# Delta rule in a one-core block: block coefficients and decay rows copied through DRAM, one direction solved from its far end, two substitutions in turn

## The chip, the cores and the metric

The kernel runs on 1 core of one Trainium2 chip, in one launch. The metric is the device time in microseconds. A core has TensorE (PE, weight loads PEld), VectorE (DVE), ScalarE (ACT), GpSimd (POOL) and SyncE (SP), and 16 DMA engines. The granted TensorE clock was 0.999 of full speed over the whole profiled run.

## What is computed

Two transformer blocks in a row over 256 tokens of 2048 channels, in float32. The second block mixes with a gated delta rule and a Fourier branch, and the change lies in the delta rule. Per head (8 heads, both directions, chunks; the kernel takes each 128 tokens as a chunk):

```
diff = gc[..., :, None] - gc[..., None, :]          # gc: running sum of the log decays g
decay = jnp.where(incl, jnp.exp(jnp.where(incl, diff, 0.0)), 0.0)
m = jnp.where(strict, jnp.einsum("bhnid,bhnjd->bhnij", kb, k) * decay, 0.0)
a_mat = m + jnp.eye(CHUNK, dtype=m.dtype)
sol = lax.linalg.triangular_solve(a_mat, rhs, left_side=True, lower=True, unit_diagonal=True)
qk = jnp.where(incl, jnp.einsum("bhnid,bhnjd->bhnij", q, k) * decay, 0.0)
...
o_b = flip(gated_delta_rule_chunked(flip(q), flip(k), flip(v), flip(g_b), flip(beta_b)))
```

The triangular matrix of 128 is inverted in 16x16 blocks on the diagonal by substitution on VectorE, and these are joined in three levels (32, 64, 128) by matmuls.

## The kernel before

**The stream.** Nearly all of the time is matmuls with streamed weights. A unit is 128x1024 weights (512 KB): SP loads it to `raw` (one of 4 slots; the slot is free when POOL has done with it), ACT copies it rounded to `w_hi` (line 678, once PE has finished the unit 4 before), POOL writes the rest to `w_lo` (line 637), PE multiplies both (lines 2201 and 2204).

**The pairs.** The 8 heads run in 4 pairs, `p` = 0 to 3; the two heads of a pair are `ways[0]` ("one") and `ways[1]` ("other"). Each has two PSUM banks, `x_ps` and `y_ps`; its four 128x128 matrices are 2 directions by 2 chunks. In a pair PE also works through 28 units of the stream, `fill(n)` being n half units, set by hand between the steps of the pair. DVE adds up each finished group of 4 units (`group_out`, lines 1830 to 1833), which frees its bank for the group after next.

**A pair, in the order of its chain.** Convolution on DVE (line 1889), silu on ACT, transposes on PE (`to_tokens`), norms on ACT (`norms`, line 1120, ending in `vt`, line 1126) and the copy of the keys, `ks`, on DVE (line 1895). Then the steps that the change touches:

- `log_sums` on PE (line 2686): a matmul with one column of `gc_head` and the rows `gc_rows` puts gc of every token on all partitions; `log_decay` on DVE takes gc of the row off it, and adds the mask; `decays` on ACT (line 1142) takes the exponential, after `betas` of both ways.
- `grams` on PE (line 2693): the products k k and q k. They wait for `ks` of their way.
- `matrices` on DVE: product with decay (line 1912), q k and level-4 masks (1914, 1918), blocks masked (1916) and summed into rows of 16 (1921), the diagonal added (1923), and these spread out by 4 products (1928, 1930).
- `spread` on PE (lines 2699, 2701): matmuls with the 0/1 matrix `same` give every partition the 16x16 coefficients of its block, in PSUM.
- `substitution` on DVE (lines 1942, 1944): for n = 1 to 15 a product and a sum for one way, each waiting for the one before, then the same for the other way; then each way's expansion and transposes (1947, 1951, 1956).
- `level` on PE (line 2720), which waits for `tt1`, the last transpose of its way; later levels, solves, states and outputs follow, with short fills between.

Every engine works through its list in order, so what stands behind a wait waits too. ACT's list holds the `w_hi` copies 3 to 30 of the pair between its own steps.

Of the kernel before, what the change touches and what calls it, by code (L numbers as in the profile page):

```python
# [18 lines left out]
F32 = mybir.dt.float32  # L19
# [7 lines left out]
P = 128  # L27
T = 256
# [175 lines left out]
def build(nc, t, out):  # L204
    ctx = ExitStack()
    with ctx:
# [15 lines left out]
        def rounds(name, names):  # L222
# [33 lines left out]
        same = own[:, 768:896]  # L256
# [6 lines left out]
        gc_rows = b[:, 7, :, :].rearrange("p s n -> p (s n)")  # L263
        gc_head = b[:, 6, 0, 0:HN]
# [22 lines left out]
        out_done = sem("out_done")  # L287

# [63 lines left out]
        mk_dve = steps("mk_dve", ["a", "b", "c", "s", "same", "neg", "nth", "which", "pick0", "pick", "sel0", "sel"])  # L352
        sc_pe = steps("sc_pe", ["feat", "scal", "cum", "rows"])
        sc_act = steps("sc_act", ["whi", "ea", "b0", "b1", "e", "ln", "eg", "er", "rowhi"])
        sc_dve = steps("sc_dve", ["wlo", "feat", "a0", "a1", "neg", "abs", "pos", "sp", "nea", "g0", "g1", "zero", "gc", "rem", "rowlo", "ne"])
# [6 lines left out]
                        + ["one", "ks", "rn", "dsub", "dmin", "m0", "m1", "m2", "m3", "qk", "blk", "mm4", "red", "dl", "r0", "r1", "r2", "r3"]  # L362
                        + [y for n in range(1, BASE) for y in (f"pr{n}", f"su{n}")] + ["cp", "ex0", "ex1", "tt0", "tt1"]
                        + [f"l{l}{n}" for l in (4, 5) for n in range(4)] + ["u60", "u61", "vd0", "vd1", "v10", "v11", "ra", "rb", "v20", "v21",
                                                          "o", "orn", "on", "ot", "lo"]) for w in range(2)]
        dn_act = [steps(f"dn_act{w}", ["sqk", "sv", "n0", "n1", "n2", "n3", "root", "vt0", "vt", "r2", "be0", "be", "qe", "exp", "mc", "x4", "x5", "x6",
                                       "s", "qs0", "qs1", "os0", "os1", "oroot0", "oroot", "hi"]) for w in range(2)]
        dn_pe = [steps(f"dn_pe{w}", ["tr1", "gc", "gram", "mbx", "mby", "x4", "tu4", "x5", "tu5", "x6", "tu6",
# [44 lines left out]
        class Way:  # L413


            def __init__(self, w, two, both):
# [12 lines left out]
                self.low_rows, self.top_rows = both[:, 0:4 * HALF * BASE], both[:, 4 * HALF * BASE:6 * HALF * BASE]  # L429
# [4 lines left out]
                self.inv = own[:, 64 * w:64 * w + 64].rearrange("p (n i) -> p n i", n=4)  # L434
                self.prod = own[:, 128 + 64 * w:192 + 64 * w].rearrange("p (n i) -> p n i", n=4)
# [230 lines left out]
        def _(act):  # L666
# [387 lines left out]
            for g in range(FG):  # L1054
# [37 lines left out]
                if g == 6:  # L1092
                    act.wait_ge(sc_pe.sem, sc_pe.at("rows"))
                    act.wait_ge(sc_dve.sem, sc_dve.at("zero"))
                    nc.scalar.activation(gc_rows[0:HN], ps[0:HN, 0, :], ACT.Copy).then_inc(sc_act.sem, 1)

            for p in range(PAIRS):
# [123 lines left out]
                for w in ways:  # L1221
                    out_norms(w)
                fill(28, 29, 30)
# [44 lines left out]
        def _(dve):  # L1268
# [514 lines left out]
            nc.vector.tensor_tensor(same, in_block[:, 0], in_block[:, 1], ALU.add).then_inc(mk, 1)  # L1783
            dve.wait_ge(mk, done("s"))
            nc.vector.tensor_tensor(same, same, ident[:], ALU.add).then_inc(mk, 1)
# [7 lines left out]
            nc.vector.tensor_scalar(gc_head, ident[:, 0:HN], 1.0, None, ALU.mult).then_inc(mk, 1)  # L1793
            dve.wait_ge(mk, done("sel0"))
            nc.vector.tensor_scalar(gc_head[32:64], ident[32:64, 32:32 + HN], 1.0, None, ALU.mult).then_inc(mk, 1)
# [39 lines left out]
            for g in range(FG):  # L1835
# [7 lines left out]
                if g == 2:  # L1843
                    nc.vector.memset(gc_rows.bitcast(F32), 0.0).then_inc(sc_dve.sem, 1)
# [4 lines left out]
                if g == 6:  # L1849
                    dve.wait_ge(sc_act.sem, sc_act.at("rowhi"))  # L1850
                    nc.vector.tensor_tensor(gc_rows[32:40], ps[0:HN, 0, :], gc_rows[0:HN].bitcast(F32), ALU.subtract).then_inc(sc_dve.sem, 1)
# [7 lines left out]
            for p in range(PAIRS):  # L1859
# [39 lines left out]
                def log_decay(w):  # L1899
                    own, y = dn_dve[w.w].sem, four1(w.y_ps)  # L1900
                    from_pe(w, "gc")
                    nc.vector.tensor_tensor(y, y, per(GC, w), ALU.subtract).then_inc(own, 1)
                    after(w, "dsub")
                    nc.vector.scalar_tensor_tensor(out=y, in0=y, scalar=0.0, in1=dmask[:], op0=ALU.min, op1=ALU.add).then_inc(own, 1)

                def matrices(w):
# [7 lines left out]
                    nc.vector.tensor_tensor(dc(w.qk), two(w.x_ps[:, T:2 * T]), dc(w.decay), ALU.mult).then_inc(own, 1)  # L1914
                    after(w, "m3")
                    nc.vector.tensor_tensor(dc(w.x), dc(y), in_block.unsqueeze(2).broadcast_to([P, 2, 2, P]), ALU.mult).then_inc(own, 1)
                    after(w, "qk")
                    nc.vector.tensor_tensor(dc(w.mm4), dc(y), lmask[:, 4].unsqueeze(2).broadcast_to([P, 2, 2, P]), ALU.mult).then_inc(own, 1)
                    after(w, "blk")
                    sums = w.x_ps[:, 0:64].rearrange("p (n i) -> p n i", n=4)  # L1920
                    nc.vector.tensor_reduce(sums, w.x.rearrange("p n (b i) -> p n i b", i=BASE), AX.X, ALU.add).then_inc(own, 1)
                    after(w, "red")
                    nc.vector.tensor_tensor(sums, sums, nth.unsqueeze(1).broadcast_to([P, 4, BASE]), ALU.add).then_inc(own, 1)
                    after(w, "dl")
                    for rows, cols, part in ((slice(HALF, BASE), BASE, w.low_rows), (slice(0, HALF), HALF, w.top_rows)):
                        place = part.rearrange("p (d c o q) -> p d c o q", d=2, c=2, o=HALF)
                        wide = [P, 2, HALF, cols]
                        nc.vector.tensor_tensor(place[:, 0], sums[:, 0:2, rows].unsqueeze(3).broadcast_to(wide),
                                                nth[:, 0:cols].unsqueeze(1).unsqueeze(1).broadcast_to(wide), ALU.mult).then_inc(own, 1)
                        nc.vector.tensor_tensor(place[:, 1], sums[:, 2:4, 0:cols].unsqueeze(2).broadcast_to(wide),  # L1930
                                                nth[:, rows].unsqueeze(2).unsqueeze(1).broadcast_to(wide), ALU.mult).then_inc(own, 1)

                def substitution(w):

                    own = dn_dve[w.w].sem
                    low = w.x_ps.rearrange("p (n o q) -> p n o q", n=4, o=HALF)
                    top = w.y_ps[:, 0:4 * HALF * HALF].rearrange("p (n o q) -> p n o q", n=4, o=HALF)
                    coef = lambda n: top[:, :, n, 0:n + 1] if n < HALF else low[:, :, n - HALF, 0:n + 1]
# [107 lines left out]
                for w in ways:  # L2046
                    matrices(w)
# [823 lines left out]
```

## Time and profile before

| | us |
|---|---|
| median of 3 runs | 2162.88 (2162.18 to 2163.45) |
| the profiled run | 2162.75 |
| its span, first to last instruction | 2160.9 |
| PE busy | 2147.3 (99%) |
| POOL busy | 1710.2 (79%) |
| DVE busy | 1088.4 (50%) |
| ACT busy | 1041.4 (48%) |
| the four pairs, about | 884 to 1268 |

Times in the rows are us from the start of the span. A row of the timeline is one instruction, or several alike in a row (x and their number), with its start and how long it took; an idle time of its engine of over 0.2 us stands in brackets, with what ended it. Matmuls overlap, so what a step costs PE is read from start to start, not from the durations.

### The profile page before, as it was taken

The numbers are of one execution on the slowest core, as the hardware profiler recorded it, in microseconds if no ns is written. First come the engines' busy times: TensorE is split into PE (matmuls) and PEld (weight loads), VectorE is DVE, ScalarE is ACT, GpSimd is POOL, SyncE is SP. The second block draws the span as 40 slices with busy tenths as digits, with TensorE's granted clock in tenths as the row PEclk, the third lists the DMA queues.
The fourth block names the chain that finished last, engine by engine and source line by source line (L and its number), as shares of the span: only waits on it lengthen the run. The fifth ranks groups of instructions, "written<-read, shape, count | busy, mean of one in ns | idle before, by whom it ended". The sixth has DMA issues, their size and how long they took to land.

```text
span 2160.9 us, 35017 instructions
## 1 busy us (share of the span) xinstructions
PE 2147.3 (99%) x12871; PEld 1847.3 (85%) x12871; DVE 1088.4 (50%) x1887; ACT 1041.4 (48%) x1533; POOL 1710.2 (79%) x729
## 2 busy tenths in 40 slices
PE   9999999999999999999999999999999999999998
PEld 8888889888888888888888888888888888888886
DVE  5994343115754253668686745118506704822842
ACT  5434455444567556646455654453333333333343
POOL 7888868877666886667676768888888888888886
PEclk9999999999999999999999999999999999999999
DMA  7666545656454765555565546656666666666664
GB/s 247 186 189 191 177 154 175 190 156 186 146 145 146 236 181 148 141 155 166 138 174 138 157 150 200 206 184 189 190 194 189 191 194 188 191 192 190 191 189 153
DMA packets 321604, 383.84 MB, mean 178 GB/s; under 512 B 14942, under 2 KB 255941, under 8 KB 321221
## 3 DMA queue, kind: packets, MB, share of 16 engines
q1 hardware_dynamic: 317269, 378.06, 58.8%
q10 hardware_dynamic: 4208, 4.00, 0.6%
q8 instruction: 90, 1.47, 0.3%
q14 instruction: 37, 0.30, 0.0%
HBM read 379.92 MB, written 2.10 MB: 177 GB/s over the span
## 4 chain that ended last, share of the span: by engine, by line
PE 97%; DVE 1%; issue 1%; ACT 1%; POOL 0%; ACTq 0%; POOLq 0%; DVEq 0%
PE lin_ps L2201 37%; PE lin_ps L2204 18%; PE lin_ps L2228 10%; PE lin_ps L2229 10%; PE lin_ps L2227 10%; PE ps L2164 1%; PE lin_ps L2411 1%; PE lin_ps L2409 1%; PE lin_ps L2410 1%; PE ps L2554 0%; DVE ps L1889 0%; POOL w_lo L637 0%; PE lin_ps L2340 0%; PE lin_ps L2341 0%; PE lin_ps L2339 0%
## 5 line engine op out<-in xcount | busy, mean ns | idle before, releaser
L637 POOL TENSOR_TENSOR w_lo<-raw,w_hi 128x1024 fp32r<-128x1024 f32 (+1 forms) x712 | 1699.2, 2396 | 426.2 <-ACT w_hi L678 318.0
L2201 PE MATMUL lin_ps<-a,w_hi 128*128 128x512 f32 x2176 | 695.0, 401 | 1.1 <-DVE a L1299 0.4
L678 ACT ACTIVATE w_hi<-raw 128x1024 fp32r<-128x1024 f32 (+1 forms) x452 | 471.1, 1053 | 450.4 <-PE lin_ps L2204 236.6
L2204 PEld LDWEIGHTS lin_ps<-a,w_lo 128*128 128x128 f32 x2176 | 408.7, 188 | 96.4
L2201 PE MATMUL lin_ps<-b,w_hi 128*128 128x512 f32 x1376 | 432.7, 396 | 0.8 <-DVE z L1534 0.8
L2204 PE MATMUL lin_ps<-a,w_lo 128*128 128x256 f32 x2176 | 428.4, 278 | 0.0
L689 ACT ACTIVATE w_hi<-raw 128x1024 fp32r<-128x1024 f32 x228 | 242.0, 1062 | 385.6 <-PE lin_ps L2204 226.4
L2201 PEld LDWEIGHTS lin_ps<-a,w_hi 128*128 128x128 f32 x2176 | 332.9, 189 | 5.5 <-issue 2.5
L2204 PEld LDWEIGHTS lin_ps<-b,w_lo 128*128 128x128 f32 x1376 | 258.5, 188 | 61.0
L2227 PE MATMUL lin_ps<-w_hi,a 128*128 128x512 f32 x752 | 293.3, 390 | 0.0
L2229 PE MATMUL lin_ps<-w_hi,a 128*128 128x512 f32 x752 | 292.7, 389 | 0.0
L2228 PE MATMUL lin_ps<-w_lo,a 128*128 128x512 f32 x752 | 292.6, 389 | 0.0
L2204 PE MATMUL lin_ps<-b,w_lo 128*128 128x256 f32 x1376 | 270.4, 278 | 0.0
L2201 PEld LDWEIGHTS lin_ps<-b,w_hi 128*128 128x128 f32 x1376 | 209.8, 189 | 1.9 <-DVE z L1534 1.3
L2229 PEld LDWEIGHTS lin_ps<-w_hi,a 128*128 128x128 f32 x752 | 141.2, 188 | 29.1
L2227 PEld LDWEIGHTS lin_ps<-w_hi,a 128*128 128x128 f32 x752 | 141.2, 188 | 29.0
L2228 PEld LDWEIGHTS lin_ps<-w_lo,a 128*128 128x128 f32 x752 | 141.2, 188 | 28.9
L1319 DVE SCALAR_TENSOR_TENSOR x<-lin_ps,nst,x 128x512 f32<-128x512 f32 x24 | 16.9, 747 | 219.6 <-PE lin_ps L2229 219.6
L2116 DVE TENSOR_TENSOR a<-scr,a 128x512 f32 x32 | 92.3, 2884 | 4.7
L1426 DVE SCALAR_TENSOR_TENSOR ps<-z,vec,ps 128x254 f32<-128x254 f32 (+28 forms) x232 | 88.4, 465 | 0.0
L2112 DVE SCALAR_TENSOR_TENSOR scr<-scr 128x512 f32<-128x512 f32 x32 | 86.8, 2714 | 1.1
L2114 DVE CAST a<-scr 128x512 f32 x32 | 78.2, 2444 | 5.1 <-DVE scr L2112 5.1
(440 smaller groups left out, 2136.7 us busy)
## 6 DMA issues: line engine op xcount, KB each, us to landing
raw<-in_w_in SPq DMA_DIRECT2D x144, 512.0 KB, 3.7
raw<-in_w_mlp_up SPq DMA_DIRECT2D x128, 512.0 KB, 3.8
raw<-in_w_mlp_down SPq DMA_DIRECT2D x128, 512.0 KB, 3.7
raw<-in_even_w_in SPq DMA_DIRECT2D x111, 512.0 KB, 3.6
raw<-in_odd_w_in SPq DMA_DIRECT2D x40, 512.0 KB, 3.7
raw<-in_even_w_out SPq DMA_DIRECT2D x32, 512.0 KB, 4.2
raw<-in_odd_w_out SPq DMA_DIRECT2D x32, 512.0 KB, 4.8
raw<-in_w_o SPq DMA_DIRECT2D x32, 512.0 KB, 4.3
```

The costliest lines, as they stand in the source:

```text
L637: nc.gpsimd.tensor_tensor(w_lo[:, slot, 0:width], raw[:, slot, 0:width], w_hi[:, slot, 0:width].bitcast(F32), ALU.subtract).then_inc(lo_do ...
L678: nc.scalar.activation(w_hi[:, slot, 0:width], raw[:, slot, 0:width], ACT.Copy).then_inc(hi_done, 1)
L689: nc.scalar.activation(w_hi[:, slot], raw[:, slot], ACT.Copy).then_inc(hi_done, 1)
L1426: nc.vector.scalar_tensor_tensor(out=acc[c][:, k:T], in0=u[c][:, 0:T - k], scalar=per_channel(w + 8 * (TAPS - 1 - k) + c), in1=acc[c][:, k:T],
L2112: nc.vector.scalar_tensor_tensor(out=tm2, in0=tmp, scalar=0.0, in1=tmp, op0=ALU.max, op1=ALU.mult).then_inc(ml_dve.sem, 1)
L2114: nc.vector.tensor_copy(bb[:, :, 0, :], tm2).then_inc(ml_dve.sem, 1)
L2116: nc.vector.tensor_tensor(bb[:, :, 1, :], tm2, bb[:, :, 0, :].bitcast(F32), ALU.subtract).then_inc(ml_dve.sem, 1)
L2201: nc.tensor.matmul(lin_ps[:, 2 * parity + m, :], hi[:, k, m * P:(m + 1) * P], src[:, kk].rearrange("p s n -> p (s n)"), start=(q == 0 and ...
L2204: last = nc.tensor.matmul(lin_ps[:, 2 * parity + m, 0:T], lo[:, k, m * P:(m + 1) * P], src[:, kk, 0, :], start=False, stop=(q == n - 1 and ...
L2227: nc.tensor.matmul(acc, ah, hi[:, k, :], start=(j == 0 and k == 0), stop=False)
L2228: nc.tensor.matmul(acc, ah, lo[:, k, :], start=False, stop=False)
L2229: last = nc.tensor.matmul(acc, al, hi[:, k, :], start=False, stop=(j == 7 and k == 1))
```

## The change

It replaces the matmuls that spread data over partitions by copies through DRAM. The cumulative log decays are written once to `gc_far` (8 rows of 512) and read back for each way, broadcast to 128 partitions (256 KB). The block rows are written to `co_far` (32 KB a way and pair) and read back so that the 16 partitions of a block all hold its 16 rows (512 KB, into the former `tu` space, now `coef`). `log_sums`, `spread`, the two helpers `gc_rows` and `gc_head`, and the four spreading products go. PE's fills 2, 9 and 13 become one of 24. One direction is solved from its last row back, so that both directions read the same rows; the sums, the inverse and the products lie in PSUM. On DVE `scales` and `log_decay` alternate by way, `group_out` of a group moves behind the coefficients of both ways, and the two substitutions alternate step by step. On ACT `decays` of the first way moves ahead of `betas`.

```diff
@@ ACT @@
+                    nc.scalar.activation(scr[0:HN, 3, :], ps[0:HN, 0, :], ACT.Copy).then_inc(sc_act.sem, 1)
+                    act.wait_ge(sc_act.sem, sc_act.at("rows"))
+                    act.dma_start(gc_far, scr[0:HN, 3, :]).then_inc(gc_out, 16)
...
+                def decay_rows(w, k):
+                    act.dma_start(w.x.rearrange("p a n -> p (a n)"),
+                                  gc_far[2 * k + w.w:2 * k + w.w + 1, :].broadcast_to([P, 4 * P])).then_inc(gc_in[w.w], 16)
+                def coefs_out(w):
+                    from_dve(w, "dl")
+                    act.dma_start(co_far[w.w], w.rows.rearrange("p n i -> p (n i)")).then_inc(co_out[w.w], 16)
+                def coefs_in(w):
+                    act.wait_ge(co_out[w.w], 16 * (p + 1))
+                    act.dma_start(w.coef, co_far[w.w].rearrange("(b o) f -> b (o f)", o=BASE).unsqueeze(1)
+                                  .broadcast_to([P // BASE, BASE, 4 * BASE * BASE])).then_inc(co_in[w.w], 16)
...
                     act.wait_ge(bld, 4)
+                    act.wait_ge(gc_out, 16)
+                    for w in ways:
+                        decay_rows(w, 0)
...
                 norms(other)
+                decays(one_way)
                 betas(one_way)
                 fill(9)
                 betas(other)
-                decays(one_way)
+                decays(other)
                 fill(10, 11)
-                decays(other)
+                coefs_out(one_way)
                 fill(12)
+                coefs_out(other)
+                fill(13)
+                coefs_in(one_way)
                 keep_m(one_way)
-                fill(13, 14)
                 keep_m(other)
+                coefs_in(other)
+                fill(14)
...
+                if p < PAIRS - 1:
+                    for w in ways:
+                        decay_rows(w, p + 1)
@@ DVE @@
+                    dve.wait_ge(gc_in[w.w], 16 * (p + 1))
+                    from_act(w, "vt")
+                    for n in range(4):
+                        nc.vector.tensor_scalar(y[:, n, :], w.x[:, n, :], col(GC, n // 2, n % 2, w), 0.0, ALU.subtract, ALU.min).then_inc(own, 1)
+                    after(w, "dsub3")
+                    nc.vector.tensor_tensor(y, y, dmask[:], ALU.add).then_inc(own, 1)
...
+                    nc.vector.tensor_reduce(w.sums, w.x.rearrange("p n (b i) -> p n i b", i=BASE), AX.X, ALU.add).then_inc(own, 1)
+                    after(w, "red")
+                    nc.vector.tensor_tensor(w.rows, w.sums, nth.unsqueeze(1).broadcast_to([P, 4, BASE]), ALU.add).then_inc(own, 1)
...
+                def substitutions():
+                    for w in ways:
+                        dve.wait_ge(co_in[w.w], 16 * (p + 1))
+                    for n in range(1, BASE):
+                        far = BASE - 1 - n
+                        for w in ways:
+                            after(w, f"su{n - 1}" if n > 1 else "one")
+                            nc.vector.tensor_tensor(window(w.prod, 0, 2 * BASE, n + 1),
...
+                        for w in ways:
+                            after(w, f"pr{n}")
+                            nc.vector.tensor_reduce(window(w.inv, far, 2 * BASE - far + n, 1), window(w.prod, 0, 2 * BASE, n + 1),
+                                                    AX.X, ALU.add).then_inc(dn_dve[w.w].sem, 1)
...
-                for step in (scales, log_decay):
+                    scales(w)
+                    log_decay(w)
+                for w in ways:
+                    blocks_of(w)
+                group_out(7 * p + 1)
+                for w in ways:
+                    masked(w)
+                group_out(7 * p + 2)
+                substitutions()
+                for step in (inverses, turned):
                     for w in ways:
                         step(w)
@@ PE @@
-                log_sums(one_way)
-                fill(2)
-                log_sums(other)
                 grams(one_way)
                 grams(other)
-                fill(9)
-                spread(one_way)
-                spread(other)
-                fill(13)
+                fill(24)
```

**PE, pair 0, around `grams`.** Lines 2201 and 2204 (2227 and 2230 in the changed kernel) are the stream, 2686 is `log_sums` of the other way, 2693 (2711) `grams` of both. Before:

```order
L2201 MATMUL lin_ps<-a,w_hi 128x512 x2
L2204 MATMUL lin_ps<-a,w_lo 128x256 x2
L2686 MATMUL ps<-b 128x512
L2693 MATMUL ps<-z 128x128 x8
L2201 MATMUL lin_ps<-a,w_hi 128x512 x2
```

Changed:

```order
L2227 MATMUL lin_ps<-a,w_hi 128x512 x2
L2230 MATMUL lin_ps<-a,w_lo 128x256 x2
L2711 MATMUL ps<-z 128x128 x8
L2227 MATMUL lin_ps<-a,w_hi 128x512 x2
L2230 MATMUL lin_ps<-a,w_lo 128x256 x2
```

`grams` now follows straight on the third half unit after the transposes, two half units earlier than before.

**ACT, pair 0, from the exponentials (1142; 1147) to the levels (1150; 1169).** Lines 678 (682) are the stream, 1146 (1165) `keep_m`, 1156 and 1160 the DMAs of the coefficients. Before:

```order
L1142 ACT_TABLE_LOAD
L1142 ACTIVATE z<-ps 128x512
L678 ACTIVATE w_hi<-raw 128x1024 x2
L1142 ACTIVATE z<-ps 128x512
L678 ACTIVATE w_hi<-raw 128x1024
L1146 ACTIVATE z<-ps 128x512
L678 ACTIVATE w_hi<-raw 128x1024 x2
L1146 ACTIVATE scr<-ps 128x512
L678 ACTIVATE w_hi<-raw 128x1024 x7
```

Changed:

```order
L1147 ACTIVATE z<-ps 128x512
L682 ACTIVATE w_hi<-raw 128x1024 x2
L1156 DMA co_far<-own 128x64
L682 ACTIVATE w_hi<-raw 128x1024
L1156 DMA co_far<-own 128x64
L682 ACTIVATE w_hi<-raw 128x1024
L1160 DMA z<-co_far 128x1x1024
L1165 ACTIVATE z<-ps 128x512
L1165 ACTIVATE scr<-ps 128x512
L1160 DMA scr<-co_far 128x1x1024
L682 ACTIVATE w_hi<-raw 128x1024 x8
```

Four DMAs stand between the copies of the stream now; the second read is issued behind both `keep_m`.

**DVE, pair 0, where the substitution begins.** Lines 1830 to 1833 (1854 to 1857) are `group_out`; 1942 and 1944 (1962 and 1967) the products and sums. Before:

```order
L1830 TENSOR_TENSOR z<-lin_ps,by_row 128x512
L1831 TENSOR_TENSOR lin_ps<-lin_ps,by_row 128x2x256
L1833 TENSOR_TENSOR z<-lin_ps,z 128x512
L1942 TENSOR_TENSOR own<-ps,own 128x4x2
L1944 TENSOR_REDUCE own<-own 128x4
L1942 TENSOR_TENSOR own<-ps,own 128x4x3
```

Changed:

```order
L1854 TENSOR_TENSOR z<-lin_ps,by_row 128x512
L1855 TENSOR_TENSOR lin_ps<-lin_ps,by_row 128x2x256
L1857 TENSOR_TENSOR z<-lin_ps,z 128x512
L1962 TENSOR_TENSOR ps<-z,ps 128x4x2
L1962 TENSOR_TENSOR ps<-scr,ps 128x4x2
L1967 TENSOR_REDUCE ps<-ps 128x2x2 x2
L1962 TENSOR_TENSOR ps<-z,ps 128x4x3
```

The two ways take turns now, so that between an instruction and the one that needs its result stands one of the other way; 60 instructions remain.

## Rows read from the trace of the kernel before

**Rows 1.** The page: busy time by engine, and the chain that ended last.

```profile
PE 2147.3 (99%) x12871; PEld 1847.3 (85%) x12871; DVE 1088.4 (50%) x1887; ACT 1041.4 (48%) x1533; POOL 1710.2 (79%) x729
...
PE 97%; DVE 1%; issue 1%; ACT 1%; POOL 0%; ACTq 0%; POOLq 0%; DVEq 0%
```

**Rows 2.** Timeline of PE, pair 0, spread: start us, us, engine, line, operation.

```profile
918.90 1.02 PE L2699 MATMUL ps<-z,own 128*128 128x512 f32 x2
...
921.30 0.81 PE L2201 MATMUL lin_ps<-a,w_hi 128*128 128x512 f32 x2
```

**Rows 3.** Timeline of PE, pair 0, from the first log_sums to grams.

```profile
901.25 0.40 PE L2686 MATMUL ps<-b 128*128 128x512 f32 x1
901.49 0.63 PE L2201 MATMUL lin_ps<-a,w_hi 128*128 128x512 f32 x2
...
904.52 1.95 PE L2693 MATMUL ps<-z 128*128 128x128 f32 x16
906.23 0.70 PE L2201 MATMUL lin_ps<-a,w_hi 128*128 128x512 f32 x2
```

**Rows 4.** Timeline of DVE: copy ks of the other way, pairs 0 and 1.

```profile
902.57 0.42 DVE L1895 COPY z<-ps 128x256 f32<-128x256 f32 x1 [2.47 <-ACT z L1120]
...
996.41 0.43 DVE L1895 COPY z<-ps 128x256 f32<-128x256 f32 x1 [2.47 <-ACT z L1120]
```

**Rows 5.** Timeline of PE: pair 1 log_sums, and first level of pairs 0 and 1.

```profile
939.70 0.45 PE L2720 MATMUL ps<-z 32*32 32x32 f32 x32
...
997.72 0.40 PE L2686 MATMUL ps<-b 128*128 128x512 f32 x1
...
1036.08 0.45 PE L2720 MATMUL ps<-z 32*32 32x32 f32 x32
```

**Rows 6.** Timeline of ACT, pair 0, from norms of the other way to fill 10.

```profile
902.90 0.63 ACT L1126 ACTIVATE z<-ps,stat 128x128 f32<-128x128 f32 x2
...
904.37 1.04 ACT L678 ACTIVATE w_hi<-raw 128x1024 fp32r<-128x1024 f32 x1
...
906.37 1.28 ACT L1142 ACT_TABLE_LOAD   x1
...
908.15 2.00 ACT L678 ACTIVATE w_hi<-raw 128x1024 fp32r<-128x1024 f32 x2
```

**Rows 7.** Timeline of POOL, pair 0: w_lo of unit 9.

```profile
905.57 2.39 POOL L637 TENSOR_TENSOR w_lo<-raw,w_hi 128x1024 fp32r<-128x1024 f32 x1 [1.50 <-ACT w_hi L678]
```

**Rows 8.** Timeline of DVE, pair 0: independent instructions in a row, and the other steps.

```profile
885.18 4.77 DVE L1889 SCALAR_TENSOR_TENSOR ps<-z,vec,ps 128x254 f32<-128x254 f32 x12
...
908.29 1.13 DVE L1912 SCALAR_TENSOR_TENSOR ps<-ps,dsc,z 128x128 f32<-128x128 f32 x4 [0.21 <-ACT z L1142]
...
911.13 1.07 DVE L1921 TENSOR_REDUCE ps<-z 128x64 f32<-128x512 f32 x1
912.23 0.23 DVE L1923 TENSOR_TENSOR ps<-ps,own 128x64 f32<-128x64 f32 x1
...
918.82 0.68 DVE L1830 TENSOR_TENSOR z<-lin_ps,by_row 128x512 f32<-128x512 f32 x1
```

**Rows 9.** Timeline of DVE, pair 0: first, last instruction and transposes of one substitution.

```profile
920.75 0.16 DVE L1942 TENSOR_TENSOR own<-ps,own 128x8 f32<-128x8 f32 x1
...
927.35 0.22 DVE L1944 TENSOR_REDUCE own<-own 128x4 f32<-128x64 f32 x1
...
928.54 0.76 DVE L1956 STREAM_TRANSPOSE z<-z 128x256 f32<-128x256 f32 x2
```

**Rows 10.** DMA issues: out<-in, queue, count, KB each, median us from issue to landing.

```profile
raw<-in_w_in SPq DMA_DIRECT2D x144, 512.0 KB, 3.7
...
z<-in_final_norm ACTq DMA_DIRECT2D x1, 1024.0 KB, 7.7
...
dmask<-in_c_dmask ACTq DMA_DIRECT2D x1, 128.0 KB, 5.3
ident<-in_c_ident ACTq DMA_DIRECT2D x1, 64.0 KB, 1.8
```

More of the change, by code:

```diff
@@ L287, in build @@
         out_done = sem("out_done")
+        gc_out = sem("gc_out")
+        gc_in = [sem(f"gc_in{w}") for w in range(2)]
+        co_out = [sem(f"co_out{w}") for w in range(2)]
+        co_in = [sem(f"co_in{w}") for w in range(2)]
+        gc_far = nc.dram_tensor("gc_far", (HN, 4 * P), F32, kind="Internal").ap()
+        co_far = [nc.dram_tensor(f"co_far{w}", (P, 4 * BASE), F32, kind="Internal").ap() for w in range(2)]
         bld = sem("bld")
@@ L428, in __init__ @@
                 self.rhs = both
-                self.low_rows, self.top_rows = both[:, 0:4 * HALF * BASE], both[:, 4 * HALF * BASE:6 * HALF * BASE]
+                self.coef = both
                 self.t, self.u = self.tu[:, 0:4, :], self.tu[:, 4:8, :]
@@ L433, in __init__ @@
                 self.x = four(two[7])
-                self.inv = own[:, 64 * w:64 * w + 64].rearrange("p (n i) -> p n i", n=4)
-                self.prod = own[:, 128 + 64 * w:192 + 64 * w].rearrange("p (n i) -> p n i", n=4)
+                self.sums, self.inv, self.prod = (self.x_ps[:, 64 * k:64 * k + 64].rearrange("p (n i) -> p n i", n=4) for k in range(3))
+                self.rows = own[:, 64 * w:64 * w + 64].rearrange("p (n i) -> p n i", n=4)
                 self.norm = stat[:, 32 + 8 * w:40 + 8 * w]
@@ L1900, in log_decay, with blocks_of @@
                     own, y = dn_dve[w.w].sem, four1(w.y_ps)
[L1901 to L1906, printed above, removed]
+                    dve.wait_ge(gc_in[w.w], 16 * (p + 1))
[4 more added lines that the diff above has]
+                    nc.vector.tensor_tensor(y, y, dmask[:], ALU.add).then_inc(own, 1)
+                def blocks_of(w):
                     own, x, y = dn_dve[w.w].sem, four1(w.x_ps), four1(w.y_ps)
@@ L1917, in matrices, with masked @@
+                    after(w, "red")
+                    nc.vector.tensor_tensor(w.rows, w.sums, nth.unsqueeze(1).broadcast_to([P, 4, BASE]), ALU.add).then_inc(own, 1)
+                def masked(w):
+                    own, y = dn_dve[w.w].sem, four1(w.y_ps)
+                    nc.vector.tensor_tensor(dc(w.qk), two(w.x_ps[:, T:2 * T]), dc(w.decay), ALU.mult).then_inc(own, 1)
                     after(w, "qk")
                     nc.vector.tensor_tensor(dc(w.mm4), dc(y), lmask[:, 4].unsqueeze(2).broadcast_to([P, 2, 2, P]), ALU.mult).then_inc(own, 1)
-                    after(w, "blk")
@@ L1920, in matrices @@
[L1920 to L1931, printed above, removed]
@@ new lines, in inverses, with turned @@
+                def inverses(w):
+                    own = dn_dve[w.w].sem
+                    after(w, f"su{BASE - 1}")
+                    wide = [P, 4, P // BASE, BASE]
+                    nc.vector.tensor_tensor(w.t.rearrange("p c (b i) -> p c b i", i=BASE), w.inv.unsqueeze(2).broadcast_to(wide),
+                                            which.unsqueeze(2).unsqueeze(1).broadcast_to(wide), ALU.mult).then_inc(own, 1)
+                def turned(w):
+                    after(w, "ex")
+                    for d in range(2):
+                        nc.vector.transpose(w.u[:, 2 * d:2 * d + 2, :].rearrange("p c n -> p (c n)"),
+                                            w.t[:, 2 * d:2 * d + 2, :].rearrange("p c n -> p (c n)")).then_inc(dn_dve[w.w].sem, 1)
@@ L2040, in _ @@
                 for w in ways:
-                    nc.vector.tensor_reduce(w.inv, nth.unsqueeze(1).broadcast_to([P, 4, BASE]).unsqueeze(3), AX.X, ALU.add).then_inc(dn_dve[w.w].sem, 1)
-                for step in (scales, log_decay):
+                    scales(w)
[8 more added lines that the diff above has]
+                for step in (inverses, turned):
                     for w in ways:
                         step(w)
-                group_out(7 * p + 1)
-                for w in ways:
-                    matrices(w)
-                group_out(7 * p + 2)
-                for w in ways:
-                    substitution(w)
                 group_out(7 * p + 3)
@@ L2695, in grams @@
                     m.then_inc(dn_pe[w.w].sem, 1)
-                def spread(w):
-                    from_dve(w, "r3")
-                    nc.tensor.matmul(w.x_ps, same, w.low_rows, start=True, stop=True).then_inc(dn_pe[w.w].sem, 1)
-                    from_act(w, "mc")
-                    nc.tensor.matmul(w.y_ps[:, 0:4 * HALF * HALF], same, w.top_rows, start=True, stop=True).then_inc(dn_pe[w.w].sem, 1)
                 def squares(l, n):
```

66 lines of the change are left out of this document (14 added, 52 removed).

## The prediction

> **What bounds the kernel now.** The page comes first: PE is busy 99% of the span and makes 97% of the chain that ended last [rows 1]. DVE is at 50% and ACT at 48%, so their work as such costs nothing. POOL at 79% is the next to watch, since each unit of the stream passes through it. So the change is worth what it takes from PE's list, less what PE comes to wait for. That is read from PE's timeline in a pair (what stands between two matmuls of the stream), and then from the timelines of ACT, POOL and DVE for what each step needs.
>
> **1. What PE no longer does.** In pair 0 the four matmuls of `spread` begin at 918.90 and the stream goes on at 921.30: 2.40 us [rows 2]. A `log_sums` stands from 901.25 to 901.49, 0.24 us, twice in a pair [rows 3]. Together 2.88 us a pair, and 11.5 us in the four pairs. Half units and the other matmuls stay, in number and shape. All of it lies on PE's path, so it is all gained unless PE waits.
>
> **2. `grams` comes two half units earlier.** A half unit takes 1.40 us (from 901.49 to 904.52, less one `log_sums`, is two). `grams` of both ways takes 1.71 us (904.52 to 906.23), 0.86 a way [rows 3]. It now starts where the first `log_sums` started. In pair 0 that is 901.25, and the second way's part is due at 902.1. But it needs `ks` of the other way, which ends at 902.99 [rows 4]. With 0.05 for the hand-over PE waits 0.95 us. In pair 1 the place is 997.72 [rows 5] and the second way is due at 998.6, behind `ks` at 996.84 [rows 4]: no wait. Pairs 2 and 3 repeat pair 1 (pair 0 alone starts right after the Fourier branch). On DVE `log_decay` of the first way now stands ahead of this `ks`: four products of 128x128, 1.13 us as line 1912 [rows 8], and a pass over 512 columns, 0.68. DVE was idle 2.47 us in front of `ks` [rows 4], which takes these 1.8 us. Without that cover each us more would be a us of PE. The decay rows themselves are read a whole tail of a pair ahead (in pair 0 ahead of 5 us of convolution [rows 8]), and cost nothing.
>
> **3. Unit 9 of pair 0 comes late.** ACT does the first exponential before `betas` now. Norms of the other way end at 903.53; the table load takes 1.28, the exponential 0.5 (to 908.15 it was 1.78 for both), `betas` about 1.0 (copy of unit 9 and one `betas` are 2.0, from 904.37 to 906.37) [rows 6]. So the copy of unit 9 starts at 906.3 instead of 904.37. POOL began 1.2 us behind ACT and took 2.39 [rows 7]: ready at 909.9. PE wants it 4 half units behind `grams`, which ends at 901.25 + 0.86 + 0.95 + 0.86 = 903.9, so at 909.5. It waits 0.45 us with the hand-over. For units 10 to 12 POOL runs without a break, 2.4 us a unit against PE's 2.8, so the wait isn't repeated. In pair 1 the same sums give 1003.8 (norms end 0.96 behind the start of `ks`, as in pair 0) against a need at 1005.0: covered by 1.2 us. The two DMAs for the next pair's decay rows add an issue each to ACT at a pair's end; half a us each is still hidden behind units already copied.
>
> **4. The coefficients: a chain in place of `spread`.** What is late next is the first level, which needs the transposes of both ways. PE gets there in pair 0 at 903.9 + 0.45 + 24 x 1.40 + 0.27 (the step into small matmuls: 906.23 to 939.70 less 22 halves and 2.40) = 938.2, before 939.70 [rows 3, 5]. In pairs 1 to 3 it is 2.88 before 1036.08, 1033.2 in pair 1 [rows 5].
> DVE in pair 0: products from 906.1, when the first `betas` is done; 1.13 + 0.68 (masked) + 1.07 (sums) + 0.23 (diagonal) with short waits between [rows 8] gives `dl` at 909.3 for the first and 912.4 for the other way. `group_out` takes 1.93 (918.82 to 920.75 [rows 8, 9]), to 914.4; the other masks are 1.5 us a way, the second way's level-4 mask at 917.3. ACT: copies 10 and 11 to 910.6, first write, copy 12, second write at 912.5, copy 13 at 913.9 (its weights land later, since POOL freed the slot later) to 914.9, first read, both `keep_m` (the second waits for the mask until 917.3), second read issued at 918.0. A write of 32 KB isn't in the trace: 64 KB took 1.8 us and 128 KB 5.3 [rows 10]. At 3 us (small, but among weight loads) it hides behind copy 12 and 13; even at 5.3 the second read moves by 0.2 us. A read of 512 KB: the weights take 3.7, the broadcast of 1024 KB 7.7 [rows 10]. I take 6.5, nearer to the broadcast, which it is like in form: landed at 924.5. DVE's next `group_out` waits for unit 11 (918.2) and ends at 920.2, so the DMA decides when the substitution begins.
> The substitution keeps its 60 instructions. One way took 6.82 us for 30, each waiting for the one before (920.75 to 927.57) [rows 9]. Independent ones overlap: 12 of 0.48 us take 4.77 with waits for results three back, so 0.09 is saved each, and four of 0.35 take 1.13 [rows 8]. Bounds for both ways: 7 us (two chains side by side) and 13.6 (nothing gained). I take 8, near the lower one, because the convolution has waits too and overlaps. Expansion (a pass of 512 columns a way) and one way's two transposes (0.76 [rows 9]) are 2.0 us. Ready at 934.5 against 938.2 in pair 0: 3.7 us to spare. In pair 1 the second read goes out at about 1011.5 by the same steps (`grams` ends at 999.4), lands at 1018.0, and the transposes end at 1028.0 against 1033.2: 5.2 us to spare. With both upper bounds (7.7 and 13.6) it is 941.3 against 938.2 and 1034.8 against 1033.2.
> A rule speaks against this edit. The sums, the inverse and the products move to PSUM. The product of 64 columns on PSUM took 0.23 us, the sum of 64 in SBUF 0.22 [rows 8, 9]: no difference, so none is in the sum. The Trainium skill (VectorE: DVE Perf Modes, on the TRN2 errata) gives VectorE 58 cycles fixed from SBUF and 120 from PSUM. By it the 60 instructions would take up to some 3.9 us longer, an estimate from that page; 3.7 us to spare would be used up in pair 0, and the total would be 0.2 us worse. The trace doesn't agree for these shapes.
>
> **Sum.** Pair 0: 2.88 - 0.95 - 0.45 = 1.5. Pairs 1 to 3: 2.88 each, 8.6. Together 10.1 us. The profiled run took 2162.75 (span 2160.9 and 1.85 around it), 0.13 below the median 2162.88, so the two are alike: 2162.9 - 10.1 = 2152.8.
>
> **Rivals.**
> A. Part of it is given back at the first level, because the substitution gains nothing from taking turns (13.6) and the read takes 7.7: waits of 3.1 in pair 0 and 1.6 in three pairs, 7.9 together, 2160.7: within 0.2%. For it: nothing in the trace overlaps at these small sizes. Against: rows 8.
> B. The two reads run into each other, the second ending 15.4 us (twice 7.7) behind the issue of the first at 914.9. With 8 us of substitution PE waits 930.3 + 10.0 - 938.2 = 2.1 in pair 0 and (first read at 1009.0) 1.2 in the others, 5.7 together: 2158.5. For it: the weight loads use the same engines, and the first read is only 3 us old. Against: two weight loads issued 2.4 us apart land 3.7 us after their issue.
> The Trainium skill (DMA: Bandwidth & Descriptors, on why a DMA increments its semaphore by 16) has a DMA use only as many engines as divide the slowest dimension of both sides. The read's source is 8 blocks by 16 copies, so it would run on 8 of the 16, with as much on each engine as in the broadcast of 1024 KB; that would end as B does. No row shows an engine's share, so the chance of B isn't built on it.
> C. Slower. The same place and mechanism, once both hold: PE stands in front of the first level until coefficients read over 15.4 us and 13.6 us of substitution are through. 930.3 + 15.6 = 945.9 is 7.7 late in pair 0, 1024.4 + 15.6 = 1040.0 is 6.8 late in the others: 28.1 - 10.1 = 18 slower, 2180.9. It decides from 24 us between the issue of the second read and the last transpose; my sum has 16.5. Against: it takes both bounds at once.
> D. More is gained: no stall in pair 0, since the second `ks` or the copy comes earlier than summed, 11.5 us, 2151.4.
>
> **How the numbers follow.** Forecast 0.62, D 0.05, B (and anything between 2155 and 2158.5) 0.14, A 0.08, C 0.11. The range holds forecast, D and B, 0.81: from 2150.8 (D with 0.6 for the runs) to 2159.0. A kernel like this is told from no change from about 0.2%, 4.3 us: faster below 2158.6, slower above 2167.2. So faster 0.62 + 0.05 + 0.14 = 0.81, same 0.08, slower 0.11.
>
> **What the profile after would show.** No line of `spread` or `log_sums` on PE; PE's busy time down by some 11 us and still 99% of the span. In pair 0 an idle time of 0.9 us within `grams`, ended by DVE's copy, and one of 0.4 at unit 9, ended by POOL; none in pairs 1 to 3. The coefficient reads land within 7.7 us of their issue; the substitution of both ways takes 7 to 9 us; DVE is idle in front of it, ended by the DMA; and PE isn't idle in front of its first level. A first level more than 24 us behind the second read would make the prediction wrong, as would POOL falling behind the stream beyond unit 12.

## The result, and the profile after

The changed kernel takes 2176.24 us (median of 4 runs, 2174.48 to 2177.72) against 2162.93 us for the kernel before (2162.18 to 2163.45): 13.3 us slower. The ratio is 1.0062, with a 95% interval of 1.0050 to 1.0074. The forecast was 10 us faster. Its profiled run took 2175.30 us, with a span of 2173.3, which is 12.4 above the span before.

The page of the changed kernel, busy time by engine and the chain that ended last, as [rows 1]:

```profile
PE 2142.9 (99%) x12831; PEld 1845.0 (85%) x12831; DVE 1061.3 (49%) x1857; ACT 1041.1 (48%) x1533; POOL 1710.0 (79%) x729
...
PE 88%; ACT 3%; DVE 3%; DMA 2%; issue 2%; POOL 2%; ACTq 0%; POOLq 0%; SPq 0%; DVEq 0%
```

The busy shares hardly differ from [rows 1], and would say that nothing happened. The chain says otherwise: PE's part of it fell from 97% to 88%, and DMA, which wasn't in it, has 2%. What PE waited for in the four pairs (880 to 1290 us; tile and line, what ended the wait, us in total, times, longest):

```profile
PE lin_ps L2227 <- POOL w_lo L641: 14.1, 5, 3.7
PE ps L2741 <- issue: 2.4, 2, 1.5
PE ps L2711 <- DVE stat L1917: 0.8, 1, 0.8
```

The five waits are at the stream of weights. None is at the first level (line 2732), where the forecast and three of its rivals looked for the next bottleneck. PE's timeline shows four long ones, one in each pair, and the short one ahead of the first:

```profile
927.25 0.73 PE L2227 MATMUL lin_ps<-a,w_hi 128*128 128x512 f32 x2 [0.21 <-POOL w_lo L641]
...
933.92 1.19 PE L2227 MATMUL lin_ps<-a,w_hi 128*128 128x512 f32 x2 [3.61 <-POOL w_lo L641]
...
939.18 0.78 PE L2227 MATMUL lin_ps<-a,w_hi 128*128 128x512 f32 x2
...
1034.85 0.99 PE L2227 MATMUL lin_ps<-a,w_hi 128*128 128x512 f32 x2 [3.73 <-POOL w_lo L641]
...
1134.79 1.19 PE L2227 MATMUL lin_ps<-a,w_hi 128*128 128x512 f32 x2 [3.15 <-POOL w_lo L641]
...
1234.64 0.70 PE L2227 MATMUL lin_ps<-a,w_hi 128*128 128x512 f32 x2 [3.35 <-POOL w_lo L641]
```

POOL is only the last link. Follow it back: POOL waited for ACT's copy (its timeline, pair 0):

```profile
931.42 11.73 POOL L641 TENSOR_TENSOR w_lo<-raw,w_hi 128x1024 fp32r<-128x1024 f32 x5 [4.22 <-ACT w_hi L682]
```

And ACT, in its timeline of the same pair, waited for the weights themselves:

```profile
913.79 0.69 ACTq L1160 DMA_DIRECT2D z<-co_far  x1
...
917.70 0.61 ACTq L1160 DMA_DIRECT2D scr<-co_far  x1
918.40 1.06 ACT L682 ACTIVATE w_hi<-raw 128x1024 fp32r<-128x1024 f32 x1
923.67 1.06 ACT L682 ACTIVATE w_hi<-raw 128x1024 fp32r<-128x1024 f32 x1 [4.20 <-DMA raw<-in_w_in]
930.20 1.06 ACT L682 ACTIVATE w_hi<-raw 128x1024 fp32r<-128x1024 f32 x1 [5.47 <-DMA raw<-in_w_in]
```

The view of the weight loads' own line, issued from 905 to 935 us (smallest, median and largest time from issue to landing), shows what became of them. Before, the same stretch (907 to 933) had 3.6/3.7/4.9. After:

```profile
DMA to landing us min/median/max: 3.7/8.0/13.1
```

**The clock.** Behind the wait PE ran at half speed for a while. The stretches 926 to 930, 930 to 934 and 934 to 938 us of the changed kernel (busy us and instructions of PE, PEld, DVE, ACT, POOL; granted clock; DMA share; GB/s):

```profile
926.00:930.00 4.00, 3.79 (x22) 3.15 (x21) 0.00 (x0) 0.00 (x0) 1.20 (x1) 1.00 0.78 177
930.00:934.00 4.00, 0.39 (x4) 0.21 (x2) 3.52 (x32) 3.16 (x3) 2.58 (x2) 0.84 0.52 180
934.00:938.00 4.00, 4.00 (x13) 3.42 (x14) 4.00 (x30) 1.07 (x2) 4.00 (x2) 0.50 0.62 150
```

The granted clock is at 0.50 in the last one, the lower level of 1.2 GHz. A unit, which is two half units, took 5.26 us (933.92 to 939.18) where it otherwise takes 2.79. The same followed the waits of pairs 1 and 2, but not the one of 3.35 us in pair 3. Read from the lengths of the units, it cost 2.6, 1.7 and 2.9 us.

**The sum, closed.** From start to start, less what a step takes without a wait, the waits for weights are 4.3 in pair 0 (both waits), then 3.9, 3.3 and 3.5, together 15.0. The clock took 7.1. `grams` in pair 0 waited 1.0, and gaps put down to issue among the small matmuls of the levels are 0.7 longer than before. Less the 11.5 of the matmuls that are gone, this makes 12.3; the spans differ by 12.4.

### The profile page after: what moved, and what is told of

It is laid out like the page before. It is cut to its first block, busy times and chain, and to the rows that moved or that the text cites. A ratio compares the mean times of both kernels' runs of the same rounds, so it can differ in the third digit from the quotient of the medians.

```text
span 2173.3 us, 34934 instructions
## 1 busy us (share of the span) xinstructions
PE 2142.9 (99%) x12831; PEld 1845.0 (85%) x12831; DVE 1061.3 (49%) x1857; ACT 1041.1 (48%) x1533; POOL 1710.0 (79%) x729
## 4 chain that ended last, share of the span: by engine, by line
PE 88%; ACT 3%; DVE 3%; DMA 2%; issue 2%; POOL 2%; ACTq 0%; POOLq 0%; SPq 0%; DVEq 0%
PE lin_ps L2227 33%; PE lin_ps L2230 16%; PE lin_ps L2255 10%; PE lin_ps L2253 10%; PE lin_ps L2254 10%; DMA raw<-in_w_in 2%; POOL w_lo L641 2%; DVE ps L1909 1%; ACT w_hi L682 1%; PE ps L2190 1%; PE ps L2580 0%; PE lin_ps L2366 0%; PE lin_ps L2367 0%; PE lin_ps L2365 0%; PE lin_ps L2503 0%
## 5 line engine op out<-in xcount | busy, mean ns | idle before, releaser
L2227 PE MATMUL lin_ps<-a,w_hi 128*128 128x512 f32 x2176 | 700.0, 403 | 15.3 <-POOL w_lo L641 14.1
L2138 DVE SCALAR_TENSOR_TENSOR scr<-scr 128x512 f32<-128x512 f32 x32 | 86.2, 2693 | 1.1
```

Source lines behind the costliest of these rows:

```text
L2138: nc.vector.scalar_tensor_tensor(out=tm2, in0=tmp, scalar=0.0, in1=tmp, op0=ALU.max, op1=ALU.mult).then_inc(ml_dve.sem, 1)
L2227: nc.tensor.matmul(lin_ps[:, 2 * parity + m, :], hi[:, k, m * P:(m + 1) * P], src[:, kk].rearrange("p s n -> p (s n)"), start=(q == 0 and ...
```

## The experiments

Seven kernels ran, each timed in turns with the kernel before (2162.4 and 2162.7 us in the two sessions).

**Is it the number of DMA engines that a read uses?** Of the changed kernel's read, 8 blocks times 16 copies times 1024 elements, the number 8 comes first. `k16` writes each way's block rows twice, so that the read can take 16 slices for 8 partitions each. What lands in SBUF is the same, from as many bytes.

```diff
-                    act.dma_start(co_far[w.w], w.rows.rearrange("p n i -> p (n i)")).then_inc(co_out[w.w], 16)
+                    for h in range(2):
+                        act.dma_start(co_far[w.w].rearrange("(b h) (o f) -> h b o f", h=2, o=BASE)[h],
+                                      w.rows.rearrange("p n i -> p (n i)")).then_inc(co_out[w.w], 16)
...
-                    act.wait_ge(co_out[w.w], 16 * (p + 1))
+                    act.wait_ge(co_out[w.w], 32 * (p + 1))
-                    act.dma_start(w.coef, co_far[w.w].rearrange("(b o) f -> b (o f)", o=BASE).unsqueeze(1)
-                                  .broadcast_to([P // BASE, BASE, 4 * BASE * BASE])).then_inc(co_in[w.w], 16)
+                    act.dma_start(w.coef, co_far[w.w].unsqueeze(1).broadcast_to([2 * P // BASE, BASE // 2, 4 * BASE * BASE])).then_inc(co_in[w.w], 16)
```

> The changed kernel, but each way's block rows are written to DRAM twice (two writes of 32 KB), so that the read's source is 16 slices by 8 copies instead of 8 by 16; the read's bytes (512 KB), its place and everything else stay. Theory E (engines): the two reads keep to 8 of the 16 DMA engines, every weight load behind them waits for its share on these 8, and PE runs out of weights; with 16 slices the weight loads issued behind a read land within 6 us of their issue instead of 9 to 13, the 3 to 3.7 us stalls of PE at the 15th to 17th unit of a pair go, so does the stretch at 1.2 GHz behind them, and the total is 2162.9 - 11.5 + 0.8 (wait for ks in pair 0) + 0.2 = 2152.5 (2151 to 2156). Theory B (bytes): 1 MB more within 17 us is too much for the DMA engines however it is spread; the stalls stay over 2 us a pair and the total is above 2165. Theory A (ACT): ACT's list with its four more DMA issues and its waits makes the units late; nothing changes, 2176.

It took 2152.22 us (2151.45 to 2153.46), ratio 0.9955 (0.9938 to 0.9971). Theory E holds, and this version beats both kernels: 10.2 us faster than the one before. PE's waits in the four pairs, all of them:

```profile
PE ps L2742 <- issue: 1.5, 2, 0.9
PE ps L2712 <- DVE stat L1918: 0.8, 1, 0.8
```

The mean granted clock is 0.999 again (0.995 in the changed kernel). The weight loads in pair 0 are still not left alone, which the expectation had partly wrong: five in a row take 6.2 to 8.5 us instead of the 6 expected, and the ring of four slots covers that, since PE has no wait for weights.

```profile
DMA to landing us min/median/max: 3.6/5.1/8.5
```

What a read takes of the DMA engines is in the DMA view of the single microsecond from 916 to 917, when the first read runs in both kernels. q10 is ACT's queue, q1 SP's with the weights; the columns are packets, MB, and share of 16 engines' time. The changed kernel:

```profile
q10 hardware_dynamic: 39, 0.16, 51.8%
q1 hardware_dynamic: 28, 0.03, 17.0%
```

`k16`:

```profile
q10 hardware_dynamic: 66, 0.27, 97.0%
q1 hardware_dynamic: 9, 0.01, 5.6%
```

The read takes about half of the engines' time in the one and nearly all in the other. A share of time doesn't count engines, but the trace also records when each engine's part of a DMA has landed. In the changed kernel each of the eight coefficient reads ends in 8 such landings (the second of pair 0 at 929.7 to 930.4 us), with one single record more about 1 us after its issue, and in `k16` each ends in 16 (923.4 to 926.1). A weight load has 16 in all kernels. Of the one issued at 917.11 in the changed kernel, 8 parts had landed by 923.5, and the other 8 landed from 927.9 to 930.2. In pair 1 it was 8 by 1023.8, and 8 from 1030.3 to 1031.1. So the weight load has landed only when its parts on the engines that also carry the reads have. That is why it is worse for the read to have half of the engines than all. From 918 to 928 us the changed kernel moved 207 GB/s in all, and `k16` 295.

The Trainium skill (DMA: Bandwidth & Descriptors, on why a DMA increments its semaphore by 16) has the slowest dimension of both sides decide how many of the 16 engines a DMA issued from ACT uses. The 8 and 16 landings agree with it, for 8 slices and for 16, and so do the 51.8% and the 97.0%.

**Is it the slices alone?** `k16` also has a second write and a slightly later read. `k8_two_writes` keeps both and takes 8 slices from the first copy:

```diff
-                    act.dma_start(w.coef, co_far[w.w].unsqueeze(1).broadcast_to([2 * P // BASE, BASE // 2, 4 * BASE * BASE])).then_inc(co_in[w.w], 16)
+                    act.dma_start(w.coef, co_far[w.w].rearrange("(b h) f -> h b f", h=2)[0].unsqueeze(1)
+                                  .broadcast_to([P // BASE, BASE, 4 * BASE * BASE])).then_inc(co_in[w.w], 16)
```

> k16 with one thing put back: the reads take their 8 slices from the first of the two copies in DRAM, 8 slices by 16 copies as in the changed kernel; both writes, all places and all bytes stay as in k16. Theory E (the number of slices sets how many DMA engines carry the read): weight loads behind a read take 9 to 13 us again, PE stalls 3 to 3.7 us in each pair, 2176 (2172 to 2178). Theory W (k16 gained by its second write or its later read, not by the slices): as k16, 2152.

It took 2171.88 us (2170.90 to 2176.08), ratio 1.0049 (1.0034 to 1.0065). Its reads end in 8 landings each again. The share of the ACT queue from 916 to 917 is 46.4%, the weight loads take up to 12.8 us, and PE waits for them in each pair:

```profile
PE lin_ps L2229 <- POOL w_lo L641: 11.8, 4, 3.8
PE ps L2743 <- issue: 2.2, 2, 1.4
PE ps L2713 <- DVE stat L1919: 0.8, 1, 0.8
```

The reads' 8 or 16 slices are all that differs from `k16`, and with them go 19.7 us. Theory W is out. With the slices the copies of each change too, from 8 to 16, and no run changes one without the other. That half of each weight load's parts still land early (in pair 1 8 by 1022.3, the other 8 from 1029.0) speaks for the engines, and against a source that is slow for all 16. The time is just below the range expected and 4.4 below the changed kernel: 2.3 of it are shorter waits (11.8 against 14.1), and the clock was low for a shorter time in pair 2. What shortened the waits is not shown.

**One read instead of two.** This kernel leaves out the second way's read, and so has wrong coefficients for half of the heads.

```diff
-                    for w in ways:
-                        dve.wait_ge(co_in[w.w], 16 * (p + 1))
+                    dve.wait_ge(co_in[0], 16 * (p + 1))
...
-                                                    window(w.coef, far * (4 * BASE + 1), 4 * BASE * n + 2 * BASE - far * (4 * BASE + 1), n + 1),
+                                                    window(ways[0].coef, far * (4 * BASE + 1), 4 * BASE * n + 2 * BASE - far * (4 * BASE + 1), n + 1),
...
                 keep_m(other)
-                coefs_in(other)
```

> The changed kernel without the read of the second way's coefficients: both substitutions use those of the first way, so half of the heads are computed wrongly; the work on every engine is the same but for this one 512 KB read a pair. Theories E and B: with half of the reads the weight load behind the first read lands about 5 us late, which the slack of the units (about 2 us in pair 0) and the ring of four slots nearly cover: stalls below 1 us a pair, 2152 to 2157. Theory A (ACT's issues and waits): the stall stays within 0.5 us of what it was, about 2174 or more.

It took 2154.04 us (2152.46 to 2155.57), ratio 0.9960 (0.9946 to 0.9975). Theory A is out, since ACT's list still has its other three DMAs and their waits. PE's waits over the four pairs, less those in front of `grams` (0.8) and at the transposes (0.2):

```profile
PE ps L2739 <- issue: 2.3, 2, 1.7
PE lin_ps L2225 <- POOL w_lo L641: 0.5, 1, 0.5
```

The slowest weight load of pair 0 still took 8.6 us. So a single read on 8 engines makes a load late by some 5 us, and the ring covers it. It is the second one that brings PE to a stop: the kernel with one read is 1.8 us above `k16`, the one with two is 22 us above that. The second read is issued 3.9 us behind the first in pair 0, before the first has landed. Our reading is that the ring has no time to fill again in between, but no run spaces the two reads out.

**The decay rows alone.** The kernel before with its `log_sums` replaced by the broadcast reads of `gc_far`, everything else as it was (the core of the edit):

```diff
-                log_sums(one_way)
                 fill(2)
-                log_sums(other)
...
+                if p < PAIRS - 1:
+                    for w in ways:
+                        decay_rows(w, p + 1)
```

> The kernel before with the decay rows alone taken through DRAM (256 KB a way and pair, broadcast), log_sums gone, and all else as before: spread, the old substitution, the order of grams and of ACT's list. If this part of the change is clean it gives 8 times 0.24 = 1.9 us: 2161.0. If broadcast reads as such hold up the weight loads, PE has idle time of over 0.5 us at the start of a pair and the total is at or above 2162.9.

It took 2162.23 us (2161.37 to 2163.69), ratio 0.9998 (0.9988 to 1.0007). That can't be told from no change, nor from the 2161.0 expected, which is 1.2 below and inside the interval. No harm of the broadcasts shows: 256 KB land in 4.1 us (median; 4.9 at most), and PE has no idle time of over 0.5 us at the start of a pair. The matmuls are gone as summed: `to_tokens` to `grams` is 0.5 us shorter in each pair. Part of it came back where nothing was changed. PE's waits in the four pairs, first before, then `rows_only`:

```profile
PE ps L2731 <- issue: 1.1, 1, 1.1
PE ps L2729 <- issue: 0.5, 1, 0.5
```

```profile
PE ps L2731 <- issue: 1.8, 2, 0.9
PE ps L2729 <- issue: 0.8, 1, 0.8
PE lin_ps L2209 <- POOL w_lo L639: 0.3, 1, 0.3
```

Together 1.3 us more. What the gaps "issue" come from is not shown by any run (more below).

**Does taking turns matter?** `k16_seq` is `k16` with all 30 instructions of one way ahead of those of the other.

```diff
-                    for n in range(1, BASE):
+                    for w, n in ((w, n) for w in ways for n in range(1, BASE)):
...
-                        for w in ways:
+                        if True:
...
-                        for w in ways:
+                        if True:
```

> k16 with the two substitutions one way after the other instead of in turn, same 60 instructions. If taking turns is what makes them short, they take 13.6 us instead of 7.2, and PE waits at its first level: 926.2 + 13.6 + 2.6 = 942.4 against 937.5 in pair 0, about 5, and 1.7, 1.9 and 2.8 in the others (1017.25, 1111.57, 1205.80 against 1031.92, 1125.98, 1219.32): 11 us more, 2163, and up to 5 us more if the clock falls behind the longest wait. If the substitution is not on the path at all: 2152. No theory on the reads differs on this.

It took 2167.35 us (2166.42 to 2169.51), ratio 1.0023 (1.0013 to 1.0032). PE's waits:

```profile
PE ps L2733 <- DVE z L1981: 10.7, 4, 4.9
PE ps L2742 <- issue: 1.7, 1, 1.7
PE ps L2712 <- DVE stat L1918: 0.8, 1, 0.8
PE ps L2733 <- DVE scr L1981: 0.4, 2, 0.2
```

11.1 us in front of the first level, as summed, and the clock fell behind three of these waits, for another 4 or so. So the substitution isn't on the path of `k16`, but there its last transpose ends only 1.6 us ahead of need in pair 0 (935.92 against 937.50). Taking turns is what keeps it off.

**The wait for `ks` in pair 0.** Two ways to get rid of it, both on `k16`. `k16_late` moves `grams` in pair 0 back by one half unit and a copy ahead of the exponential:

```diff
@@ PE @@
-                fill(3)
+                fill(3 if p else 4)
...
-                fill(24)
+                fill(24 if p else 23)
@@ ACT @@
                 norms(other)
+                fill(9)
                 decays(one_way)
                 betas(one_way)
-                fill(9)
```

> k16 with two moves against the waits of pair 0: grams one half unit later in pair 0 only (fill 4 and 23 instead of 3 and 24), and ACT's copy of unit 9 ahead of the first exponential in every pair. Theory E: the idle times of 0.8 and 0.05 us in pair 0 go too, 11.5 us in all, 2151.4, about 0.9 below k16. Theory B: as k16, above 2164.

It took 2153.36 us (2152.54 to 2154.56), ratio 0.9957 (0.9940 to 0.9973), not better than `k16`. The 0.8 is gone, and a wait for POOL of nearly its size has come up behind it, since the next copy still stands behind the exponential and both `betas`:

```profile
911.76 0.74 PE L2228 MATMUL lin_ps<-a,w_hi 128*128 128x512 f32 x2 [0.71 <-POOL w_lo L641]
```

Its profiled run also has 3.0 us of gaps put down to issue against 1.5 in `k16`, and behind one of 1.66 us in pair 1 the granted clock was 0.50 for 3.4 us.

`k16_swap` is meant to bring `ks` forward instead:

```diff
                 norms(one_way)
-                fill(8)
                 norms(other)
+                fill(8)
```

> k16 with ACT's norms of the other way ahead of its copy of unit 8 instead of behind it. The copy of the keys then ends 1.0 us earlier (901.5 instead of 902.5) and grams of the other way doesn't wait in pair 0; unit 8's rest weights are ready 1.1 us later, which its 3.4 us of slack cover. Expected: the wait of 0.82 us in pair 0 goes, 2151.4. If the 0.82 comes back as another wait (at unit 9, whose copy stands behind the exponential), 2152.2.

It took 2152.27 us (2151.59 to 2153.26), ratio 0.9951 (0.9938 to 0.9965), the same as `k16`. PE waits 0.6 at `grams` instead of 0.8, and 0.2 at a unit. `ks` didn't come 1.0 us earlier, because it didn't wait for the norms of the other way. DVE's timeline of `k16_swap` shows what stands ahead of it:

```profile
901.75 1.11 DVE L1925 TENSOR_SCALAR ps<-z,dsc 128x128 f32<-128x128 f32 x4 [0.57 <-ACT z L1131]
902.90 0.70 DVE L1927 TENSOR_TENSOR ps<-ps,dmask 128x512 f32<-128x512 f32 x1
903.51 0.41 DVE L1916 COPY z<-ps 128x256 f32<-128x256 f32 x1
```

The copy of the keys (line 1916) follows `log_decay` of the first way (1925, 1927) without idle time, and so it does in `k16` (902.04) and in the changed kernel (902.66). `log_decay` waits for `vt` of its own way, which neither edit moves. A wait of about this size stayed in both kernels, at `grams` or at a unit, and 0.8 us could hardly have been told in the times.

## Why the prediction was wrong

**What failed.** Step 4, in one respect: it asked when the coefficient reads land for the substitution that waits for them, and never what they do to the other transfers in flight. In the whole prediction the weight loads behind them have no price: that term stood at nothing, without a reason. What they had to hide in, some 2 us of slack in the units (the last one before the waits was ready at 922.0 and needed at 924.1) and four slots of `raw`, was never set against two reads of 512 KB on half of the engines. The runs showed it at 15.0 us of waits for weights and 7.1 of low clock behind them, and `k16` and `k8_two_writes` tie both to the 8 engines.

**The rule that was put aside.** Rival B cited the page by which the read uses 8 engines, and priced the second read's end at 930.3. The first product of the substitution starts when it has landed (DVE, pair 0, the changed kernel: first product, the last step, and the last transposes):

```profile
930.49 0.17 DVE L1962 TENSOR_TENSOR ps<-z,ps 128x8 f32<-128x8 f32 x1 [9.75 <-DMA scr<-co_far]
...
937.17 0.22 DVE L1962 TENSOR_TENSOR ps<-scr,ps 128x64 f32<-128x64 f32 x1
937.30 0.36 DVE L1967 TENSOR_REDUCE ps<-ps 128x4 f32<-128x64 f32 x2
...
939.45 0.73 DVE L1980 STREAM_TRANSPOSE scr<-scr 128x256 f32<-128x256 f32 x2
```

Hence B was right on the end of the reads to 0.2 us. The 0.2 is partly luck: the first read went out at 913.79 and not at 914.9, and from there to the end the two took 16.6 us and not 15.4. The forecast's 6.5 us for a read and its bound of 7.7 were too low (9.2 for the first in pair 0, 12.8 for the second). In `k16`, on 16 engines, they took 5.8 and 9.0, and the slack in front of the first level covered that too. Even so B's total of 2158.5 was 18 us off, because it let only the substitution suffer. The transposes ended at 940.18, and PE, held up by weights, got to its first level at 945.00. With weights in time it would have been there at about 938.1 (an estimate: the 937.50 of `k16`, plus the 0.6 by which its `grams` starts earlier), so that B's wait of 2.1 was there in pair 0, hidden behind the larger one. The first level stood 27.3 us behind the issue of the second read, past the 24 that the prediction named as a sign of being wrong, but the coefficients were ready after 22.5 and it was the weights that took the rest. C had the sign and about the size of the loss, by a mechanism that didn't occur, which is luck: the substitution took 7.2 us and not 13.6.

**The rest, point by point.**
- The matmuls that go: 11.5 us, and the stream closes over the gaps as summed. PE's busy time fell by 4.4 us and not by 11, since units at 1.2 GHz count as busy for longer; in `k16` it fell by 12.9.
- `grams` in pair 0: 0.95 forecast. Its two ways start 1.87 us apart instead of 0.86, so 1.0.
- The late unit in pair 0: POOL was forecast to be ready at 909.9. It was, at 909.97 (907.57, and 2.40 for one of five). PE was there at 909.78 instead of 909.5, so that some 0.25 was lost, and no idle time over 0.2 shows; 0.45 was forecast. In `k16` it is the same (start to start 0.48 instead of 0.23).
- The write of 32 KB: 3 forecast, 1.5 for the first and 3.3 for the second in pair 0.
- The substitution: 8 us forecast with bounds 7 and 13.6. Both ways took 7.17 us in turn (930.49 to 937.66) and 14.0 one after the other in `k16_seq`. Rival A is out.
- PSUM: the prediction compared a product with a sum, and both kernels' products have an operand in PSUM, the coefficients before and the inverse after, so that they can't show it. The sums moved from SBUF to PSUM as a whole. The one of 64 columns took 0.22 us before [rows 9] and 0.23 in `k16_seq`, and a chain of 30 instructions 6.82 before and 7.05 there (927.28 to 934.33). So the move costs 0.2 us a way. The Trainium skill (VectorE: DVE Perf Modes, on the TRN2 errata) gives 58 cycles for SBUF and 120 for PSUM. That difference doesn't show in these sums.

With the reads on 16 engines the forecast's sum comes out: `k16`'s 2152.2 is 0.6 below the 2152.8 of the prediction, well inside the 2 us between its own runs.

## What to carry to other kernels

A DMA has two prices: when it lands for its own consumer, and what it does to every transfer that shares engines with it. Before adding one beside a stream, look at the first dimension of both of its sides, and give it 16 slices (here by writing a small source twice). In this case transfers on half of the engines held up those that need all of them, from 3.7 us to 13. When a busy engine stays at 99% and the time still grows, read its waits and follow the last releaser back two steps: POOL was named, and a DMA was meant.

## What was not expected of the hardware

- At waits of 3.15 to 3.73 us the granted clock of PE fell to 1.2 GHz three times in the changed kernel. It did not at the wait of 3.35 us in pair 3, nor in `k8_two_writes` at one of 2.55 us there, but it did in that kernel at one of 2.26 us in pair 2. It also fell behind gaps put down to issue: of 1.74 us in `one_read` and of 1.66 in `k16_late`, both in pair 1, but not behind one of 1.70 in `k16_seq`. In `one_read` three steps of the stream then took 3.72 us instead of 2.09, so that it lost 1.6 us in the profiled run. The wait's length alone doesn't tell it. In the changed kernel the clock added half as much again to what the waits cost.
- Gaps of 0.4 to 1.7 us, put down to "issue", stand among the 32x32 matmuls of the levels in every kernel, one to three in the four pairs, and at other places in each kernel. Their sum was 1.6 us before, 2.6 in `rows_only`, 2.4 after, 1.5 in `k16` and 3.0 in `k16_late`. A change worth 2 us can disappear in them. PE goes through its instructions fastest there, which would fit a wait for the loading of its code, but no run here tests that.
